# A kernel of two transformer blocks: softmax probabilities of the second block divided ahead of their transposes, on VectorE and GpSimd

## The reference

```python
def attend(q, k, v, bias=None, mask=None, sink=None):
    s = jnp.einsum('...qngd,...knd->...ngqk', q, k).astype(jnp.float32) * (HEAD_DIM ** -0.5)
    ...
    p = jax.nn.softmax(s, axis=-1)
    if sink is not None:
        p = p[..., :-1]
    return jnp.einsum('...ngqk,...knd->...qngd', p.astype(v.dtype), v)
```

## Time and profile before

| | |
|---|---|
| time, median of 3 runs | 3769.82 us (3765.19 to 3773.6) |
| profiled execution: span from first to last instruction | 3759.3 us |
| time of the runs above that span (median less span) | 10.5 us |
| busy, share of the span | PE 97%, PEld 79%, DVE 57%, ACT 49%, POOL 47% |
| NA, first score matmul to the end of the last value | 2288.9 to 2433.5 us |
| SWA, likewise | 3185.6 to 3341.5 us |
| the chain that ended last, by engine | PE 70%, issue 16%, POOL 7%, DVE 5%, ACT 2% |

### The profile page before, as it was taken

One profiled execution on the slowest core, in us unless ns is written; L12 is line 12 of the kernel. 1 busy time (PEld: TensorE's weight loads), 2 busy tenths in 40 slices (PEclk: granted clock), 3 DMA queues, 4 the chain that ended last, 5 costly groups with the idle time before them and its releaser, 6 DMA issues.

```text
span 3759.3 us, 58539 instructions
## 1 busy us (share of the span) xinstructions
PE 3640.2 (97%) x19802; PEld 2981.0 (79%) x19802; DVE 2155.5 (57%) x3352; ACT 1841.9 (49%) x3549; POOL 1769.9 (47%) x1407
## 2 busy tenths in 40 slices
PE   9998999999999989999999999999999999999999
PEld 7866788788887767887888887788888987778887
DVE  6576642888545766338884864642236856743234
ACT  5556444444445664444344545744445653654443
POOL 4423663556543245635655362165554135035554
PEclk9999999999999999999999999999999999999999
DMA  4210241465222202425643422132223542012222
GB/s 144 90 62 29 90 141 62 162 195 174 96 90 80 72 18 101 140 66 175 194 161 103 141 84 90 46 112 95 96 94 118 178 142 73 1 46 90 97 96 87
DMA packets 106909, 388.50 MB, mean 103 GB/s; under 512 B 11856, under 2 KB 11984, under 8 KB 106320
## 3 DMA queue, kind: packets, MB, share of 16 engines
q1 hardware_dynamic: 87840, 318.81, 25.6%
q10 hardware_dynamic: 16416, 57.62, 4.6%
q0 software_dynamic: 2448, 9.36, 0.7%
HBM read 383.65 MB, written 2.10 MB: 103 GB/s over the span
## 4 chain that ended last, share of the span: by engine, by line
PE 70%; issue 16%; POOL 7%; DVE 5%; ACT 2%; DMA 0%; POOLq 0%; ACTq 0%; DVEq 0%; SPq 0%
PE ps L687 18%; PE ps L689 18%; PE ps L688 18%; POOL arena_parts L651 3%; PE ps L1174 2%; POOL arena_parts L655 1%; PE ps L1193 1%; PE ps L1182 1%; POOL lines L438 1%; PE ps L2397 1%; PE ps L859 1%; PE ps L1152 1%; PE ps L860 1%; PE ps L861 1%; PE ps L2407 1%
## 5 line engine op out<-in xcount | busy, mean ns | idle before, releaser
L688 PE MATMUL ps<-arena_parts 128*128 128x512 f32 (+1 forms) x3148 | 1172.6, 372 | 0.0
L651 POOL TENSOR_TENSOR arena_parts<-ring,arena_parts 128x512 fp32r<-128x512 f32 x492 | 654.6, 1330 | 1013.6 <-ACT arena_parts L628 806.2
L687 PE MATMUL ps<-h_parts,arena_parts 128*128 128x512 f32 x2080 | 817.5, 393 | 10.5 <-POOL arena_parts L651 7.6
L689 PE MATMUL ps<-h_parts,arena_parts 128*128 128x512 f32 x2080 | 811.7, 390 | 0.0
L655 POOL TENSOR_TENSOR arena_parts<-ring,arena_parts 128x512 fp32r<-128x512 f32 x492 | 666.1, 1354 | 292.6 <-ACT arena_parts L637 291.9
L688 PEld LDWEIGHTS ps<-arena_parts 128*128 128x128 f32 x3148 | 594.7, 189 | 103.5 <-issue 2.4
L1824 DVE SCALAR_TENSOR_TENSOR conv<-ps,cols,conv 128x511 f32<-128x511 f32 (+3 forms) x536 | 377.2, 704 | 520.3 <-ACT conv L1839 371.1
L628 ACT ACTIVATE arena_parts<-ring 128x512 fp32r<-128x512 f32 x574 | 361.1, 629 | 640.1 <-PE ps L689 597.7
L637 ACT ACTIVATE arena_parts<-ring 128x512 fp32r<-128x512 f32 x574 | 360.2, 628 | 594.4 <-PE ps L689 558.9
L687 PEld LDWEIGHTS ps<-h_parts,arena_parts 128*128 128x128 f32 x2080 | 391.5, 188 | 97.2 <-POOL arena_parts L651 8.0
L689 PEld LDWEIGHTS ps<-h_parts,arena_parts 128*128 128x128 f32 x2080 | 391.3, 188 | 81.5
(11 more groups left out here) (382 smaller groups left out, 6417.8 us busy)
## 6 DMA issues: line engine op xcount, KB each, us to landing
ring<-in_stream SPq DMA_DIRECT2D x606, 512.0 KB, 3.3
ctx<-in_mod ACTq DMA_DIRECT2D x48, 512.0 KB, 3.4
sq<-in_mod ACTq DMA_DIRECT2D x48, 512.0 KB, 3.4
sq<-in_bias POOLq DMA_DIRECT2D x8, 512.0 KB, 4.6
conv<-in_bias POOLq DMA_DIRECT2D x8, 512.0 KB, 4.7
arena<-in_mem ACTq DMA_DIRECT2D x2, 1024.0 KB, 7.6
out_y<-x ACTq DMA_DIRECT2D x8, 256.0 KB, 2.7
x<-in_x SPq DMA_DIRECT2D x4, 256.0 KB, 4.7
```

Of the source, the lines that this page charges most:

```text
L651: eng.tensor_tensor(side_of(lin, i, c, 0, to), side_of(lin, i, c, 0, raw), side_of(lin, i, c, 0, top), ALU.subtract)\
L687: pe.matmul(out, w_h, x_h, start=start, stop=False)
L688: pe.matmul(out, w_h, x_r, start=False, stop=False)
L689: return pe.matmul(out, w_r, x_h, start=False, stop=stop)
```

## The change

The division moves from the result of V to the probabilities, ahead of their transposes.

- The spreading matmuls on TensorE, the copy of their result on VectorE and the buffer `inv_row` go. The output step of VectorE becomes a plain copy out of PSUM.
- Behind the reciprocal of a unit VectorE multiplies the probabilities of head 0 by it in place (`duo_scale_dve`) and GpSimd those of head 1 (`duo_scale_pool`). For the first four units of NA (`alone=4`) VectorE takes both heads. In SWA a unit of one head is scaled by one of the two engines alone, and the reciprocal is taken for each unit and no longer once for a block.
- A third probability buffer is added to both attentions. That of NA lies in the second weight tile's high part, so that the high part of the second weight tile of the output projection is made behind the last copy of the attention and no longer ahead of it.
- T waits for the scaled probabilities of both engines, and stands one unit later on TensorE: V of n-3, T of n-1, S of n+2. VectorE's output step is one unit later too (n-4), and stands behind the reciprocal and the scaling.
- The bias DMAs of NA are issued by GpSimd between its scalings, behind that of a pair's first unit.

The core of the diff:

```diff
-        na_prob = [quarters[:, 2 * s:2 * s + 2, :].rearrange("p a b -> p (a b)") for s in range(2)]
+        na_prob = [cut(18432 + (L["o", 0].tile0 + 1) % 2 * TILE, TILE)]
+        na_prob += [quarters[:, 2 * s:2 * s + 2, :].rearrange("p a b -> p (a b)") for s in range(2)]
...
-        swa_prob = [cut(8704 + 1024 * s, 1024) for s in range(2)]
+        swa_prob = [cut(at, 1024) for at in (8704, 9728, 14336)]
...
+                    un.dve_heads = [a for a in un.heads if a == 0 or n < alone]
+                    un.pool_heads = [a for a in un.heads if a == 1 and n >= alone]
...
             def turn(n):
-                pe.wait_ge(S["p_done"], D.u0 + n + 1)
+                un = D.units[n]
+                wait(pe, "head_scaled_dve", D.dve0 + D.dve_scaled[n + 1])
+                wait(pe, "head_scaled_pool", D.pool0 + D.pool_scaled[n + 1])
                 wait(pe, "pt_ready", D.u0 + n)
...
-                pe.wait_ge(S["ri_ready"], D.inv0 + v + 1)
                 wait(pe, D.evac, v)
-                for a in range(2):
-                    mm = pe.matmul(psf[heads_of(a), INVERSE:INVERSE + P], inv2[:, v % 2, a:a + 1].to_broadcast([P, HD]), ident,
-                                   start=True, stop=True)
-                mm.then_inc(S["inv_spread"], 1)
...
-            for n in range(N):
-                if n >= 2:
-                    values(n - 2)
+            for n in range(N + 1):
+                if n >= 3:
+                    values(n - 3)
+                if n >= 1:
+                    turn(n - 1)
                 if n + 2 < N:
                     scores(n + 2)
-                turn(n)
...
+        def duo_scale_dve(dve, D, n):
+
+            un = D.units[n]
+            dve.wait_ge(S["ri_ready"], D.inv0 + n + 1)
+            for a in un.dve_heads:
+                part = D.cut(D.prob, n)[:, un.heads.index(a), :]
+                dve.tensor_scalar(part, part, inv2[:, un.block % 2, a:a + 1], None, ALU.mult).then_inc(S["head_scaled_dve"], 1)
+
+        def duo_scale_pool(pool, D, n):
+
+            un = D.units[n]
+            for a in un.pool_heads:
+                part = D.cut(D.prob, n)[:, un.heads.index(a), :]
+                pool.wait_ge(S["ri_ready"], D.inv0 + n + 1)
+                pool.tensor_scalar(part, part, inv2[:, un.block % 2, a:a + 1], None, ALU.mult).then_inc(S["head_scaled_pool"], 1)
...
         def duo_out_dve(dve, D, v):
-            block, at = D.blocks[v], D.inv0 - INV_NA + v + 1
-            dve.wait_ge(S["inv_spread"], at)
-            dve.tensor_copy(inv_row[:, :], psf[:, INVERSE:INVERSE + P]).then_inc(S["inv_row"], 1)
-            dve.wait_ge(S["inv_row"], at)
+            block = D.blocks[v]
             dve.wait_ge(S["pv_done"], D.v0 + v + 1)
-            dve.tensor_tensor(block.to, block.view(psf[:, VALUES:VALUES + P]), block.view(inv_row[:, :]), ALU.mult).then_inc(S[D.evac], 1)
+            dve.tensor_copy(block.to, block.view(psf[:, VALUES:VALUES + P])).then_inc(S[D.evac], 1)
...
-            for n in range(N + 3):
+            for n in range(N + 4):
                 if n < N:
                     top(n)
-                if n >= 3:
-                    duo_out_dve(dve, NA, n - 3)
                 if 1 <= n <= N:
                     inverse(n - 1)
+                    duo_scale_dve(dve, NA, n - 1)
+                if n >= 4:
+                    duo_out_dve(dve, NA, n - 4)
```

More of the change, by code:

```diff
@@ L2346, in by_columns, with __init__ @@
             return v.rearrange("p (r g c) -> p r g c" if natural else "p (g r c) -> p r g c", **dims)
-        TURNED, VALUES, INVERSE = 5 * 512, 7 * 512, 4 * 512
+        TURNED, VALUES = 5 * 512, 7 * 512
         class Duo:
-            def __init__(self, u0, inv0, blocks, prob, probT, evac, ready, turn_ready, value_ready={}):
+            def __init__(self, u0, inv0, blocks, prob, probT, evac, ready, turn_ready, value_ready={}, alone=0, before=None):
                 self.u0, self.inv0, self.blocks, self.evac = u0, inv0, blocks, evac
@@ L2499, in build @@
         NA = Duo(U_NA, INV_NA, na_blocks(), na_prob, na_probT, "na_evac", [("lin_free", L["v", 0].chunk0 + 1)],
-                 [("lin_free", L["v", 0].freed)], {4: ("shifted", 4)})
+                 [("lin_free", L["v", 0].freed)], {4: ("shifted", 4)}, alone=4)
         NA.v0 = U_NA
@@ L2513, in na_pool @@
                 pool.tensor_copy(v2_shifted[64:P, :, cs], v2[0:64, 1:4, cs]).then_inc(S["shifted"], 1)
-            for p in range(2, PAIRS):
-                pool.wait_ge(S["biased"], B_NA + (p - 1) * QB)
-                na_bias(pool, p)
+            pool.wait_ge(S["shifted"], 4)
+            for n in range(len(NA.units)):
+                duo_scale_pool(pool, NA, n)
+                p, at = divmod(n, NA_UNITS)
+                if at == 0 and 1 <= p < PAIRS - 1:
+                    pool.wait_ge(S["biased"], B_NA + p * QB)
+                    na_bias(pool, p + 1)
         def na_pe(pe):
@@ L2571, in na_act @@
                 if n == N - 3:
-                    first_high(act, L["o", 0])
+                    high(act, L["o", 0], 0, 0)
+            high(act, L["o", 0], 0, 1)
             high_of_pair(PAIRS - 1, False)
@@ L2663, in inverse @@
             def inverse(n):
-                v = SWA.block_done(n)
-                if v is None:
-                    return
+                v, c = SWA.units[n].block % 2, SWA.units[n].c
                 dve.wait_ge(S["p_done"], U_SWA + n + 1)
                 dve.wait_ge(S["sink_exp"], n + 1)
-                dve.tensor_tensor(sum2[:, v % 2, :], sum2[:, v % 2, :], esink[:, v % 2, :], ALU.add).then_inc(S["sum_ready"], 1)
-                dve.wait_ge(S["sum_ready"], v + 1)
-                dve.reciprocal(inv2[:, v % 2, :], sum2[:, v % 2, :]).then_inc(S["ri_ready"], 1)
+                dve.tensor_tensor(sum2[:, v, c], sum2[:, v, c], esink[:, v, c], ALU.add).then_inc(S["sum_ready"], 1)
+                dve.wait_ge(S["sum_ready"], n + 1)
+                duo_inverse_free(dve, SWA, n)
+                dve.reciprocal(inv2[:, v, c], sum2[:, v, c]).then_inc(S["ri_ready"], 1)
             def out(n):
@@ L2680, in swa_dve @@
             N, per = len(SWA.units), len(SWA.units) // PAIRS
-            for n in range(N + 3):
+            for n in range(N + 4):
                 if n < N:
                     top(n)
-                if n >= 3:
-                    out(n - 3)
                 if 1 <= n <= N:
                     inverse(n - 1)
+                    duo_scale_dve(dve, SWA, n - 1)
+                if n >= 4:
+                    out(n - 4)
                 if n % per == 4 and n > per:
@@ L3230, in _ @@
             turn_keys_pool(pool)
+            for n in range(len(SWA.units)):
+                duo_scale_pool(pool, SWA, n)
             heads_output(1, U_SWA + PAIRS * SWA_UNITS)
```

26 lines of the change are left out of this document (20 added, 6 removed).

## The result

| | before | after |
|---|---|---|
| median of 4 runs each, us | 3769.95 (3765.19 to 3773.6) | 3801.51 (3799.23 to 3804.3) |
| ratio | | 1.0092, 95% interval 1.0076 to 1.0108 |
| span of the profiled execution | 3759.3 | 3800.1 |
| ahead of NA's first scores | 2288.9 | 2294.0 |
| NA, first scores to the next stage's first matmul | 146.0 | 153.2 |

The account below looks back on a forecast made before the run. TensorE was taken to bound both attentions. Savings of 10.2 us (NA) and 6.8 (SWA) against new waits of 4.9 and 7.7 gave -4.4 on the profiled 3759.3; with 10.5 us kept to the median, 3765 us, range 3748 to 3780.

Parts of the forecast that it names:

- What bounds the kernel: Both attentions are bound by TensorE, at 17.37 us a pair in NA and 17.88 in SWA; other engines partly idle.
- the computed floor: TensorE's time for an NA pair without the spreading and without any new wait: 16.1 us.
- What goes: Removing the spreading on TensorE saves 0.21 us a block: -10.2 us in NA (48 blocks), -6.8 in SWA (32).
- GpSimd's price: GpSimd's scaling of 512 elements takes 0.7 us, bounds 0.55 and 1.33, ending 1.1 us behind the reciprocal.
- Who is first: VectorE's scaling starts ahead of GpSimd's, which waits; rival, GpSimd first or dear: 15%, with GpSimd first giving 3782 us.
- The loop in NA: In NA, ties and the late rests of a pair cost 0.7 us a pair, over 7 pairs +4.9 us.
- the tie of 4.3 us: In NA, transposes are due 4.3 us after the scores' start, and the scaled probabilities they need also take 4.3 us.
- The loop in SWA: In SWA, transposes of unit 5 wait 1.4 us a pair, 0.34 already inside: +1.1 a pair, +7.7 over 7 pairs.
- The clock: Rival: the new 1.4 us wait in each SWA pair halves TensorE's clock, 5 us each time; 3785 us, chance 8%.
- The ends: NA's end some 0.8 us shorter and its start 0.5, SWA's end +1.3; these cancel, within 3 us.

Follow-up runs that it names:

- GpSimd alone: Changed kernel, but VectorE scales head 0 in the first four units only, GpSimd head 1 by tensor_scalar as before; 3792.94 us in one run.
- two banks: Changed kernel with two result banks used in turn, so the values product waits for the copy of two blocks back; 3795.42 us, ratio 1.0063.
- mixed: Changed kernel, two result banks, both engines scaling by tensor_tensor, but VectorE alone by tensor_scalar on units of 640 keys; 3792.11 us, ratio 1.006.
- half-scaled pair of kernels: Changed kernel with GpSimd scaling only the first half of head 1's columns: 3772.23 us with one result bank, 3772.19 us with two.

## Why the prediction was wrong, point by point

**What bounds the kernel**: right. TensorE alone bounded both attentions, and without the spreading a pair fell to the computed floor (16.07 for 16.1).

**What goes**: right. 0.217 a block for 0.21 in NA; in SWA 17.88 - 17.23 = 0.65 a pair, where four times 0.21 and the 0.34 gave 1.18. There a wait of 0.55 for the exponentials was left.

**GpSimd's price: the step that failed.** "I take 0.7, bounds 0.55 and 1.33." It is 1.56 for 512 elements and 1.88 for 640, over the upper bound, which came from a subtraction of two tensors, taken to be the dearer form. It is not: 1.04 for the product of two tensors of which one is broadcast, 1.56 for tensor_scalar. With the wait for VectorE GpSimd ended 1.95 us behind the reciprocal, where 1.1 was counted. The copy of the earlier trace rows was the nearest row by its number of inputs, and of no use for the price. The 769 ns of the Trainium skill (GPSIMD Engine Reference, "Elementwise — side-by-side cycle accounting") are half of the 1.56 us that the run with GpSimd alone shows for tensor_scalar. The 36 us between forecast and result lie for 12.5 in NA (7.2 longer where 5.3 shorter was counted) and for 25.7 in SWA (26.6 where 0.9 was); together 38, by one execution each.

**Who is first**: right for this kernel, VectorE by 0.05 to 0.07. But that this decides was wrong as a reason: with GpSimd's tensor_tensor the starts were the same and VectorE waited. The Trainium skill (SBUF — State Buffer, "Who interferes with whom") says that issue order and not the form decides; by the starts that the records show, the run with GpSimd's tensor_tensor speaks against it, though the records do not show when either was issued. The same section of the Trainium skill has a VectorE instruction with two inputs in SBUF contend with a GpSimd instruction that reads SBUF; the 1.04 that became 1.55 agrees.

**The loop in NA**: the tie of 4.3 us became a miss of 0.85 by GpSimd's price, with both its own time and its wait. The prediction had 16.8 a pair and 18.34 was measured; half a scaling, 1.2 us, with two banks gives 17.06. The second step that failed is a term that was missing altogether: V waits for the output of the block before, which the new order puts behind a maximum, a reciprocal and a scaling. Without GpSimd it costs 17.48 - 16.07 = 1.4 us a pair. In the changed kernel it is hidden behind GpSimd.

**The loop in SWA**: a wait once a pair was right, its place and size were not. The count followed the both-headed units; T of unit 4 hangs on one instruction of GpSimd of 1.88 us, whose reciprocal stands behind the whole mask and maximum of unit 5. It waits 1.67; the waits at T of units 5 and 0 add 0.15 and 0.18, and the 0.33 at the scores, counted as inside, came on top. The forecast was 17.88 - 0.84 + 1.1, a pair of about 18.1, and it takes 19.13, 1.0 more. The count also overlooked a wait in its own figures: T of unit 4 was due at about 7.1 (1.28 + 1.04 + 0.7 + 1.06 + 0.7 + 1.06 + 1.23), while its reciprocal was ready at 7.15 and its scaling, by the 0.7, at 7.9. That would only have moved part of the 1.4 from unit 5 to unit 4. With GpSimd's 1.08 for half of the 640 the waits are indeed 0.87 and 0.31.

**The clock**: priced as a rival at 8%, for a wait of 1.4 us. It happened beside the first failure, and it is the largest single part of the miss: 14.7 of SWA's 26.6, by the periods above. It fell in the middle in all four kernels with a wait of 1.67 or more at a T in each pair (changed, two banks, GpSimd alone, mixed). Of the nine kernels whose steady pairs have new waits at T, none over 1.03 us, six kept the full clock in the middle, two lost it once and one twice. So no sharp line was found, and why it fell behind some of the equal waits and not behind others stays open. That the longer wait brought the falls is read from which kernels have them; no run held the clock apart from the wait. The half-scaled pair of kernels, without and with two falls at the same waits, shows again what two of 6.8 us cost: 6.3 us. That is the rate that was priced (5 for ten microseconds), at shorter falls.

**The ends**: right for NA; in SWA the first pair took 3.6 us longer than before, and the stretches ahead of its T and behind the last period 0.9. The start is bare, 1.35 us of TensorE's work in the 4 us from 3200, and the clock fell there as in before, for 13.7 us where it was 10.2. By the rate above that is some 1.5 of the 3.6, an estimate; how the rest divides stays open.

## What to carry to other kernels

An engine that has never done an operation in the trace has no nearest row: form, not the number of inputs or elements, set GpSimd's price here (1.04 or 1.56 us for the same product). Before moving a step past others, list each buffer that its old place kept free, with the instruction that frees it; here the single result bank was worth 1.4 us a pair where nothing larger hid it. And where TensorE runs without a gap, a new wait can cost more than its length: here 1.7 us in each 19 went along with 14.7 us lost to the clock.

## What was not expected of the hardware

- GpSimd: tensor_scalar of f32 takes 0.92, 1.56 and 1.88 us for 256, 512 and 640 elements, tensor_tensor with a broadcast operand 0.61, 1.04 and 1.25 (the first two with VectorE's waiting behind them). The three times of tensor_scalar and the 1.08 for 320 lie on one line: 0.28 us and 2.5 ns for each element.
- Beside VectorE's tensor_scalar (0.49 alone, 512), GpSimd's tensor_scalar takes 1.86 and VectorE's keeps its 0.49; GpSimd's tensor_tensor keeps its 1.04 and VectorE's takes 1.37, although VectorE's record starts first in both. Beside VectorE's tensor_tensor (0.69) GpSimd's takes 1.55.
- The stretch ahead of NA, the same code in all kernels, took 2287.9 to 2298.8 us.
